# Two products taken together, tile by tile, at the opening of a stage, and operands made earlier, in a two-block transformer kernel on one core

## The reference, cut to what matters

```python
u = rmsnorm(h, ffn_pre_norm[i])                       # first block, feed-forward
gate, up = jnp.split(u @ w_gate_up[i], [D_FF], axis=-1)
y = (jax.nn.silu(gate) * up) @ w_down[i]
h = h + rmsnorm(y, ffn_post_norm[i])
h = h + (p[i] @ ple_proj[i]) * jax.nn.sigmoid(h @ ple_gate[i])
...
x = x + jnp.concatenate([y_mla, y_diff], axis=-1) @ w_out[i]      # second block
x = x + conv_ffn(rms_norm(x, ffn_norm_g[i]), w_gate[i], w_up[i], conv_w[i], conv_b[i], w_down[i])
gate = jax.nn.sigmoid(rms_norm(x, ple_norm_g[i]) @ w_ple_gate[i])
x = x + gate * (p[i] @ w_ple_proj[i])
```

## Time and profile before

| what | value |
|---|---|
| time, median of 3 runs | 3400.74 us (3395.79 to 3401.58) |
| profiled execution, its own time | 3395.17 us |
| profiled execution, span of the records | 3393.8 us |
| TensorE busy | 3051.4 us, 90% of the span |
| VectorE busy | 1578.3 us, 47% |
| ScalarE busy | 1005.1 us, 30% |
| granted TensorE clock, mean over the span | 0.938 |

### The profile page before, as it was taken

The page is one execution under the profiler, slowest core; times in us unless marked ns, Lnnn a source line. Parts: engine busy times, 40 slices in busy tenths (PEclk is TensorE's granted clock), DMA queues, the critical chain, the costliest instruction groups (busy, mean ns, idle before and its releaser), DMA issues.

```text
span 3393.8 us, 35010 instructions
## 1 busy us (share of the span) xinstructions
PE 3051.4 (90%) x14748; PEld 2532.7 (75%) x14748; DVE 1578.3 (47%) x2018; ACT 1005.1 (30%) x1324; POOL 133.8 (4%) x73
## 2 busy tenths in 40 slices
PE   8988878987999999997899777788999999999988
PEld 6777766865888888885677555687877888888867
DVE  4146557634434334433541277366335454444444
ACT  3133334432211111113231266565322211211241
POOL 0011122013000000000100000000000000000000
PEclk9999988987999999998899888688999999999989
DMA  4111120020111111111121000000211111111111
GB/s 156 44 38 50 38 100 7 1 93 25 44 50 50 50 50 46 44 54 44 31 93 44 31 13 1 21 1 1 83 36 50 50 44 56 44 50 50 50 44 62
DMA packets 43211, 156.13 MB, mean 46 GB/s; under 512 B 5136, under 2 KB 5648, under 8 KB 43056
## 3 DMA queue, kind: packets, MB, share of 16 engines
q1 hardware_dynamic: 43056, 153.90, 13.8%
HBM read 136.85 MB, written 17.04 MB: 45 GB/s over the span
## 4 chain that ended last, share of the span: by engine, by line
PE 81%; DVE 10%; ACT 5%; issue 3%; DMA 0%; POOL 0%; SPq 0%; DVEq 0%; ACTq 0%
PE PS L264 21%; PE PS L266 20%; PE PS L268 20%; PE PS L427 2%; PE PS L429 2%; PE PS L428 2%; PE PS L1054 2%; PE PS L619 1%; PE PS L2173 1%; PE PS L1024 1%; PE PS L1801 1%; PE PS L1039 1%; PE PS L1771 1%; PE PS L1637 1%; PE PS L2164 1%
## 5 line engine op out<-in xcount | busy, mean ns | idle before, releaser
L258 DVE TENSOR_TENSOR w_lo<-w_raw,w_hi 128x1024 fp32r<-128x1024 f32 x215 | 271.5, 1272 | 464.0 <-ACT w_hi L252 464.0
L264 PE MATMUL PS<-u_hi_f,w_hi 128*128 128x512 f32 x1408 | 439.6, 394 | 29.4 <-DVE u_lo_f L360 22.2
L252 ACT ACTIVATE w_hi<-w_raw 128x1024 fp32r<-128x1024 f32 x215 | 226.0, 1053 | 765.4 <-PE PS L268 547.8
L266 PE MATMUL PS<-u_lo_f,w_hi 128*128 128x512 f32 x1408 | 437.0, 392 | 0.0
L268 PE MATMUL PS<-u_hi_f,w_lo 128*128 128x512 f32 x1408 | 436.6, 391 | 0.0
L264 PEld LDWEIGHTS PS<-u_hi_f,w_hi 128*128 128x128 f32 x1408 | 265.7, 190 | 90.6 <-issue 15.1
L266 PEld LDWEIGHTS PS<-u_lo_f,w_hi 128*128 128x128 f32 x1408 | 266.6, 189 | 56.0
L268 PEld LDWEIGHTS PS<-u_hi_f,w_lo 128*128 128x128 f32 x1408 | 266.4, 189 | 55.9
L264 PE MATMUL PS<-f_ah,w_hi 128*128 128x512 f32 x704 | 218.7, 392 | 10.2 <-DVE f_al L1415 10.2
L266 PE MATMUL PS<-f_al,w_hi 128*128 128x512 f32 x704 | 218.1, 391 | 0.0
L268 PE MATMUL PS<-f_ah,w_lo 128*128 128x512 f32 x704 | 218.1, 391 | 0.0
(11 more groups left out here) (357 smaller groups left out, 5069.4 us busy)
## 6 DMA issues: line engine op xcount, KB each, us to landing
w_raw<-in_weights SPq DMA_DIRECT2D x215, 512.0 KB, 3.6
H<-in_x_t SPq DMA_DIRECT2D x16, 512.0 KB, 5.4
stick_kept<-stick_stage SPq DMA_DIRECT2D x12, 512.0 KB, 2.9
mixer<-stick_kept SPq DMA_DIRECT2D x9, 512.0 KB, 7.1
h_kept<-H SPq DMA_DIRECT2D x8, 512.0 KB, 5.6
H<-h_kept SPq DMA_DIRECT2D x8, 512.0 KB, 7.1
out_t<-H SPq DMA_DIRECT2D x8, 512.0 KB, 2.9
bias_lines<-df_line SPq DMA_DIRECT2D x16, 143.9 KB, 8.7
```

Of the source, the lines that this page charges most:

```text
L252: act.activation(self.w_hi[i][:], self.w_raw[i][:], ACT.Copy).then_inc(*self.s("w_hi").up(g))
L258: dve.tensor_tensor(self.w_lo[i][:], self.w_raw[i][:], self.w_hi[i][:].bitcast(F32), ALU.subtract).then_inc(*self.s("w_lo").up(g))
L264: ins = e.matmul(banks[i], lh, rh[i], start=first, stop=False)
L266: ins = e.matmul(banks[i], lh, rl[i], start=False, stop=False)
```

## The change

Four edits. (1) `pe_first` takes products 0 and 1 together: for each tile of the operand one step of product 0 and one of product 1. The token sums are moved into product 2, behind its step 1 (in `f1` behind step 6), and the spread stands behind step 4 as before (in `f1` behind step 7). (2) In `in1` and `in2` ScalarE alternates part and square, and VectorE adds a square after each part. (3) The parts and the squares of `f2` are made inside `out2`, each tile after its addition; the operand of `f2` moves to other memory (from slot 26 to 17), and the squares get two tiles of their own. (4) The parts of `p2` are made between the copies of the embedding products; the parts of `p` move to tiles of their own. The number of matmuls, of squares and of parts is the same; there is no more table load on ScalarE than before.

```diff
-        self.uf = [[tile(f"u_hi_f{n}", 26, 8, F32R), tile(f"u_lo_f{n}", 34, 8, F32R)] for n in (1, 2)]
+        self.uf = [[tile(f"u_hi_f{n}", s, 8, F32R), tile(f"u_lo_f{n}", s + 8, 8, F32R)] for n, s in ((1, 26), (2, 17))]
...
-    def pe_first(self, tag, g, U, rows=None, by="dve"):
+    def pe_first(self, tag, g, U, rows=None, total=None, sums=1, spread=4, by="dve"):
 
         pe = self.nc.tensor
-        self.pe_product(g[0], 0, U, ready=tag, by=by)
-        self.pe_product(g[1], 1, U, by=by)
+        for i in range(2):
+            pe.wait_ge(*self.s("w_lo").at(g[i]))
+            self.claim(i, **{by: 1})
+        for k in range(KT):
+            pe.wait_ge(*self.s("u_lo").at(tag, k))
+            for i in range(2):
+                mm = self.pe_step(g[i], i, U, k, self.chunk(k), k == 0, k == KT - 1)
+                if k == KT - 1:
+                    mm.then_inc(*self.s("w_used").up(g[i]))
         if rows is None:
             self.pe_product(g[2], 2, U, by=by)
             return
-        pe.wait_ge(*self.s("sq_added").at(tag, KT - 1))
         self.claim(3)
-        self.pe_token_sums(tag, rows)
-
-        def spread(k):
-            if k == 4:
+
+        def between(k):
+            if k == sums:
+                pe.wait_ge(*self.s("sq_added").at(tag, KT - 1))
+                self.pe_token_sums(tag, rows if total is None else total)
+            if k == spread:
                 self.pe_spread(tag, rows)
 
-        self.pe_product(g[2], 2, U, between=spread, by=by)
+        self.pe_product(g[2], 2, U, between=between, by=by)
...
+    def dve_parts_squares(self, tag, U, gain, sq, total):
+
+        for k in range(KT):
+            self.dve_part(tag, k, U, self.H[:, k, :], gain[:, k:k + 1])
+            if k:
+                self.dve_square(tag, k - 1, sq, total)
+        self.dve_square(tag, KT - 1, sq, total)
...
     def pe_ffn(self, n):
-        self.pe_first(tag, [gates[0], ups[0], gates[1]], U, self.f_rows[n][:])
+        if n:
+            self.pe_first(tag, [gates[0], ups[0], gates[1]], U, self.f_rows[n][:], self.f_sums[:])
+        else:
+            self.pe_first(tag, [gates[0], ups[0], gates[1]], U, self.f_rows[n][:], sums=6, spread=7)
...
     def act_ple(self, n):
                 act.activation(pp[:, 4 * half + c, :], self.pair(c), ACT.Copy).then_inc(*self.act_frees(c, tag, half, c))
+                if n:
+                    k, i = 4 * half + c, FF_TILES // 2 - 1
+                    act.wait_ge(*self.dve_freed(self.ff_down_pair(i, k), "f2", "down", i, k))
+                    self.act_part(tag, k, U, H[:, k, :], gain[:, k:k + 1])
             self.act_split(g + RING)
...
     def dve_ple(self, n):
         for half in range(2):
+            if n:
+                for k in range(4 * half, 4 * half + 4):
+                    self.dve_part(tag, k, U, H[:, k, :], gain[:, k:k + 1])
             self.dve_split(base + half + RING)
...
     def act_out2(self):
         for j in range(KT):
             self.act_split(U_OUT2 + j + RING)
+            act.wait_ge(*self.dve_freed(j % 4, "o2y", j))
+            self.act_part("f2", j, self.uf[1], self.H[:, j, :], gain[:, j:j + 1])
+            if j >= 2:
+                act.wait_ge(*self.s("sq_added").at("f2", j - 1))
+            act.activation(self.f_sums[:] if j == 0 else self.f_square[:], self.H[:, j, :], ACT.Square).then_inc(
+                *self.s("sq").up("f2", j))
...
     def dve_out2(self):
             self.dve_split(U_OUT2 + j + RING)
+            self.dve_part("f2", j, self.uf[1], self.H[:, j, :], gain[:, j:j + 1])
+            if j:
+                dve.wait_ge(*self.s("sq").at("f2", j))
+                if j >= 2:
+                    dve.wait_ge(*self.s("sq_added").at("f2", j - 1))
+                dve.tensor_tensor(self.f_sums[:], self.f_sums[:], self.f_square[:], ALU.add).then_inc(
+                    *self.s("sq_added").up("f2", j))
```

More of the change, by code:

```diff
@@ L168, in memory @@
         self.f_conv = tile("f2_conv_in", 49)
-        self.cw = at("f2_cw", [P, 4], 4096 * 50)
+        self.f_sums, self.f_square = tile("f2_sums", 49), tile("f2_square", 50)
         self.up = [[tile(f"u_hi_p{n}", 26, 8, F32R), tile(f"u_lo_p{n}", 34, 8, F32R)] for n in (1, 2)]
         self.pp = [tile(f"p{n}_pp", 42, 8) for n in (1, 2)]
+        self.pe_parts = [[self.up[0][i][:, 6:8, :] for i in range(2)],
+                         [tile(f"p2_in_{n}", 20 + 2 * i, 2, F32R)[:] for i, n in enumerate(("hi", "lo"))]]
         self.p_s = [tile("p2_s0", 17), tile("p2_s1", 18)]
@@ L533, in dve_in1 @@
             self.dve_split(g)
-        for k in range(KT):
-            self.dve_part("in1", k, self.u1, self.H[:, k, :], gain[:, k:k + 1])
-        self.dve_squares("in1", [self.big[:, 0, :], self.big[:, 1, :]], self.rows1[:])
+        self.dve_parts_squares("in1", self.u1, gain, [self.big[:, 0, :], self.big[:, 1, :]], self.rows1[:])
         self.dve_statistics("in1", self.rows1[:])
@@ L1294, in act_ffn @@
         sg, prod = self.f_gate[n], self.f_prod[n]
-        gain = self.gain(("ffn_pre_norm", "ffn_norm_g_2")[n])
-        for k in range(KT):
-            if n == 0:
+        if n == 0:
+            gain = self.gain("ffn_pre_norm")
+            for k in range(KT):
                 self.act_wait_added(tag, k)
[L1299 to L1302, removed]
+                self.act_part(tag, k, U, self.H[:, k, :], gain[:, k:k + 1])
+            self.act_squares(tag, [sg[:], prod[:]])
         self.act_statistics(tag, self.f_rows[n][:])
@@ L1378, in dve_ffn @@
                 dve.wait_ge(*self.d(f"tile_in{k}").at("x again"))
-        for k in range(KT):
-            if n == 0:
+            for k in range(KT):
                 self.dve_add(tag, k, self.gain("attn_post_norm"))
-            self.dve_part(tag, k, U, self.H[:, k, :], gain[:, k:k + 1])
-        self.dve_squares(tag, [sg[:], prod[:]], rows[:])
+                self.dve_part(tag, k, U, self.H[:, k, :], gain[:, k:k + 1])
+            self.dve_squares(tag, [sg[:], prod[:]], rows[:])
         self.dve_statistics(tag, rows[:])
@@ L1479, in act_ple @@
                 act.activation(pp[:, 4 * half + c, :], self.pair(c), ACT.Copy).then_inc(*self.act_frees(c, tag, half, c))
+                if n:
+                    k, i = 4 * half + c, FF_TILES // 2 - 1
+                    act.wait_ge(*self.dve_freed(self.ff_down_pair(i, k), "f2", "down", i, k))
+                    self.act_part(tag, k, U, H[:, k, :], gain[:, k:k + 1])
             self.act_split(g + RING)
-        gain = self.gain("ple_norm_g_2")
-        for k in range(KT):
-            if n == 0:
+        if n == 0:
+            for k in range(KT):
                 self.act_wait_added(tag, k)
[L1485 to L1490, removed]
+                self.act_part(tag, k, U, H[:, k, :], 1.0)
+        else:
             self.act_squares(tag, [self.p_s[0][:], self.p_s[1][:]])
@@ L1517, in dve_ple @@
             dve.wait_ge(*self.act_freed(3, "f1 out", "rows"))
-        gain = self.gain("ple_norm_g_2")
-        for k in range(KT):
-            if n == 0:
+            for k in range(KT):
                 self.dve_add(tag, k, self.gain("ffn_post_norm"))
-            self.dve_part(tag, k, U, H[:, k, :], gain[:, k:k + 1] if n else 1.0)
-        if n:
+                self.dve_part(tag, k, U, H[:, k, :], 1.0)
+        else:
             self.dve_squares(tag, [self.p_s[0][:], self.p_s[1][:]], self.p_rows[:])
@@ L1591, in dve_in2 @@
         dve, gain = self.nc.vector, self.gain("attn_norm_g_2")
-        for k in range(KT):
-            self.dve_part("in2", k, self.u2, self.H[:, k, :], gain[:, k:k + 1])
-        self.dve_squares("in2", [self.res[:, 0, :], self.res[:, 1, :]], self.rows2[:])
+        self.dve_parts_squares("in2", self.u2, gain, [self.res[:, 2, :], self.res[:, 3, :]], self.rows2[:])
         self.dve_statistics("in2", self.rows2[:])
@@ L2269, in dve_out2 @@
             self.dve_channels("o2", k, k % 4, self.uo2, self.gout8[:, k:k + 1])
+        gain = self.gain("ffn_norm_g_2")
         for j in range(KT):
```

45 lines of the change are left out of this document (27 added, 18 removed).

## The result

The changed kernel takes 3375.07 us (median of 4 runs, 3372.89 to 3378.29) against 3398.33 us of the kernel before (4 runs, 3395.79 to 3401.58): 23.3 us less, a ratio of 0.993 with a 95% interval of 0.9915 to 0.9945. The forecast was 3375. The profiled execution took 3374.64 us; its span is 3373.3 us at a mean clock of 0.941, where before had 3393.8 at 0.938.

A forecast was written before the change was run, and what follows sets the result against it. PE's work plus its waits was taken to bound the kernel. Gains of 9.5, 3.1, 5.3 and 6.1 us sum to 24.0, giving 3371.2 from the profiled execution or 3376.7 from the upper heap; it said 3375, range 3366 to 3384.

The forecast's parts named there:

- `p1`: 9.5 forecast: `p1` opening: products 0 and 1 fill PE's idle time, leaving two steps (2.86 us) after the last tile; gain 9.5 us.
- `f2`: 5.3 forecast: `f2` opening: idle of 3.81 us and low-clock restart of 1.5 both go, the operand being ready early; gain 5.3 us.
- `p2`: 6.1 forecast: `p2` opening: the 4.61 us wait and the low-clock first steps (4.20 instead of 2.72 us) go; gain 6.1 us.
- `f1`: 3.1 forecast: `f1` opening: fourth product starts 4.95 us earlier, less 1.9 for a low-clock restart; net gain 3.1 us (2.5 to 3.6).
- rival A: Last two steps of `p1` and `f1` both run at low clock, 2.4 us each lost; about 3380 us; chance 0.10.
- That chain: `f1`, spread's start to fourth product: scale's copy, first result's emptying and weight split, outside PE, take 7.57 us as before.
- B: One stage's gain is eaten by the next wait, in `p1` through late weights; 3385 to 3391 us; chance 0.05.
- C: Alternating products run at 1.2 GHz throughout, seen in `f2`'s first 20 us; slower, up to 3465 us; chance 0.02.
- D: Alternating part and square in `in1` and `in2` switches ScalarE's tables, 13 us lost per stage; 3403 us; chance 0.01.
- the openings of `in1` and `in2`: PE is the slow engine there, 2.72 us per tile against VectorE's 2.43; gain nothing, at worst first tiles slip 1 us.

The follow-up runs named there:

- the last experiment: The kernel with `p2`'s early input, plus six of `p1`'s eight operand tiles made between the copies out of the embedding products: 3327.38 us.
- the early sums: The changed kernel with `f1`'s token sums behind step 1 and its spread behind step 4 of product 2, in place of 6 and 7: 3376.99 us.
- the early split: The changed kernel with the fourth product's weight split ahead of the statistics in `f1`, `f2` and `p2`: 3358.71 us.
- `p2`'s early input: The kernel with the early split, plus `p2`'s input `p` loaded and split before the last down products, into memory of its own: 3350.99 us.

## Why the prediction was right, point by point

**The sum.** Forecast 9.5 + 3.1 + 5.3 + 6.1 = 24.0 us, measured 23.3. By the trace the four terms are 9.5 + 2.2 + 4.5 + 8.2 = 24.4 us: the mechanism and the sum were right, and the errors of three terms cancel. That the time itself came out at 3375.07 for a forecast of 3375 is luck. The forecast lay between two bases, on "two heaps" of four times; 29 later runs of before fill the range from 3394.35 to 3407.87 with no such heaps, and the four of after spread over 5.4 us. The predicted terms, read in the trace of after:

`p1`: 9.5 forecast, 9.46 measured, and product 2 begins 1650.15 - 1647.30 = 2.85 us after the last tile's first matmul, as forecast (2.86). The work did move into PE's idle time.

`f2`: 5.3 forecast, 4.01 + 1.53 = 5.5 measured up to the fourth product. `p2`: 6.1 forecast; 5.31 up to the opening and 1.49 in it are 6.8, of which 0.7 are in the embedding products. Both rest on the same reading: the idle and the restart behind it go together.

What the forecast left out in both is the restart behind the wait for the fourth product's weights, which it took to stay as it is. In `f2` the wait is 5.57 us in both kernels, but four steps from there take 2554.10 - 2545.69 = 8.41 us now, seven pairs of them slow, and took 2565.33 - 2557.91 = 7.42: 1.0 us lost, so `f2` gives 4.5.

```profile
2565.33 0.61 PE L264 MATMUL PS<-u_hi_f,w_hi 128*128 128x512 f32 x2
```

`f1`: 3.1 forecast, 2.2 measured. This term was mis-sized, and by rival A. The step was "From the start of the spread to the fourth product ... So the fourth product starts at 859.5 + 7.57 = 867.1". That chain was right: 872.13 - 864.45 = 7.68 us. What was not was the start of the spread, 864.45 - 819.71 = 44.7 us after the opening and not 859.5 - 815.85 = 43.7, because of the end of the pass. The tile at 841.34 came after 2.30 us of idle, and the pairs behind it took 0.93 to 1.05 us. Between it and the last tile PE doesn't wait again, so nothing takes up this loss: PE reached the last tile's steps at 848.52, 28.8 us after the opening, where the forecast has the last tile at 843.44 - 815.85 = 27.6. That is 1.2 us late. The forecast put A's price at both last steps running low in `f1` and `p1` alike; what happened is a loss two tiles earlier, and in `f1` alone. From the last tile to the fourth product it is 872.13 - 848.52 = 23.6 us (forecast 23.7). The wait grew to 5.69 us as forecast (5.7), and the restart behind it cost 1.6 (forecast 1.9).

**Off the forecast to the good.** In `p2` the fourth product waits 3.05 us now as before (3.06), but came back at full clock, 0.73 in place of 1.22 us for the first pair: 1.4 us that no term had. With the 0.7 us in the embedding products it makes up for the 0.9 us that `f1` and the 0.8 us that `f2` fell short by. No run shows why this restart went away and that of `f2` grew.

**The rivals.** A happened in small, in one stage. B: the gain wasn't eaten; in `p1` no wait for weights came. C, alternating products at 1.2 GHz: the first 14 steps of `f2` take 2522.78 - 2503.74 = 19.04 us, 1.36 a step, so no. D, table switches: none, and without edit 2 the time is the same, so the alternation costs nothing and brings nothing. For the forecast that edit 2 and the openings of `in1` and `in2` are worth nothing, this is the test; the 0.7 us in the table above are within what stretches without any edit show.

**What stays open.** The profiled executions differ by 20.5 us, the medians by 23.3, the rows of the table at the edited openings by 3.8 - 1.6 + 9.5 + 4.0 + 0.5 + 5.3 + 2.9 = 24.4. Between 24.4 and 20.5 lie 6.6 us lost in the two attention stretches, which no edit touches, and 2.5 gained in three small rows. Over the kernels of this study the first of these stretches comes out between 1.2 us shorter and 5.3 us longer than in before. What decides that wasn't settled.

## What to carry to other kernels

Price an idle of the bounding engine with the slow steps that follow it: here the slow restarts behind a wait of 3.05 to 7.7 us cost 1.4 to 2.8 us on top, and in the last experiment the restarts were 6.0 of 19.8 us; but count that price only where no later wait takes it up. When an opening is made shorter, look which chain on the other engines now ends last and see whether a link of it (here the weight split) can go ahead of the statistics; that was worth 16.4 us, more than any of the four edits. And work for a next stage fits best between the copies of the stage that feeds it, as long as those copies wait for TensorE anyway.

## What the runs showed that was not expected

Where in a pass the clock falls matters more than whether it falls. In `f1` PE stands about 2.3 us before two tiles, 13.6 and 21.6 us after the opening. In after, the first wait is followed by pairs at full clock (0.73, then 0.62), and the second by the slow ones. It was so with edit 1 alone, without edit 2, with the early sums, with the early split and in the last kernel. The pass then ends 1.2 us late each time. In the kernel with `p2`'s early input it was the first of the two, and the second wait shrank to 0.88 us and took the loss up:

```profile
835.10 1.22 PE L271 MATMUL PS<-u_hi_f,w_hi 128*128 128x512 f32 x2 [2.29 <-DVE u_lo_f L375]
...
843.18 0.74 PE L271 MATMUL PS<-u_hi_f,w_hi 128*128 128x512 f32 x2 [0.88 <-DVE u_lo_f L375]
```

Its `f1` is 1.0 us shorter for it. In `p1` the same two places decide between 9.5 us, as in after, where the slow pairs came at 1633.49, and 8.3 us in the kernel with the early split, where they came behind the second wait, two tiles (8 us) later:

```profile
1626.22 0.73 PE L270 MATMUL PS<-u_hi_p,w_hi 128*128 128x512 f32 x2 [2.23 <-DVE u_lo_p L374]
...
1634.20 0.90 PE L270 MATMUL PS<-u_hi_p,w_hi 128*128 128x512 f32 x2 [2.24 <-DVE u_lo_p L374]
```

The first pair doesn't tell it alone: in the kernel with early sums it takes 0.75 us at 839.02, and the next four 1.03 to 1.06. And the same wait of 3.05 us before the fourth product of `p2` ends at 1.22 us in before (first row) and with edit 1 alone (second), and at 0.73 or 0.74 in all five kernels that have edits 3 and 4 and the weight split in its old place, after among them:

```profile
3330.26 1.22 PE L264 MATMUL PS<-u_hi_p,w_hi 128*128 128x512 f32 x2 [3.06 <-DVE w_lo L258]
```

```profile
3323.02 1.22 PE L264 MATMUL PS<-u_hi_p,w_hi 128*128 128x512 f32 x2 [3.05 <-DVE w_lo L258]
```

After 4.6 us of idle and more, every restart in the openings was at 1.2 GHz (1.19 to 1.22 us for the first pair).
